# Weight buffers moved by 16 bytes under an unchanged stream of matmuls

## The reference

```python
u = rms_norm(h, g_norm) @ w_in              # 2048 x 8192, columns q, f, i, z
...
h = h + (o * jax.nn.silu(z)) @ w_out        # 2048 x 2048
...
u = rms_norm(h, g_kv) @ w_kv                # 2048 x 4112
...
sub = jnp.einsum("thpc,hpnc->thpn", qh, peer_sub_keys)
v1, i1 = lax.top_k(sub[:, :, 0], 16)
...
h = jnp.einsum("cd,chkd->chk", xc, jnp.take(peer_u, ec, axis=0))
a = jax.nn.gelu(h, approximate=False) * gc
y = jnp.einsum("chk,chkd->cd", a, jnp.take(peer_v, ec, axis=0))
```

## The kernel before

| tensor | byte | modulo 64 |
|---|---|---|
| `e_coef_hi` | 22240 | 32 |
| `wlo`, `raw` | 24416 | 32 |
| `gap` (unused, 576 bytes) | 57184 | 32 |
| `token` | 57760 | 32 |
| `whi` | 57856 | 0 |
| `hT` | 74240 | 0 |
| `xb` high, low | 91648, 109056 | 0, 0 |
| `xa` high, low | 126464, 143872 | 0, 0 |
| `e_coef_lo` | 144128 | 0 |
| `e_coef_first` | 228096 | 0 |

## Time and profile before

### The profile page before, as it was taken

How to read it: one execution, slowest core, us unless ns; L and a number is a source line. 1 busy time by engine, 2 the same in 40 slices (tenths; PEclk the granted TensorE clock), 3 DMA queues, 4 the chain that set the end, 5 groups by cost and what they waited for, 6 DMA issues and landing times.

```text
span 3083.3 us, 63457 instructions
## 1 busy us (share of the span) xinstructions
PE 3026.1 (98%) x25252; PEld 2947.4 (96%) x25252; DVE 1885.8 (61%) x3274; ACT 1629.6 (53%) x2604; POOL 667.0 (22%) x292
## 2 busy tenths in 40 slices
PE   8999999999999999989999999999999999999999
PEld 7999998999999998869999989999999999999999
DVE  5555556744544558767777788654457865554554
ACT  5766766566678743565444443444444444444443
POOL 3333333444444333214444400000000000000000
PEclk9999999999999999999999999999999999999999
DMA  5444443454444454415555544555554455555554
GB/s 192 148 139 147 141 145 123 168 175 164 164 139 145 139 184 150 137 55 191 178 179 185 182 138 139 187 185 187 189 190 165 152 180 190 189 181 188 190 190 163
DMA packets 72288, 506.67 MB, mean 164 GB/s; under 512 B 7904, under 2 KB 10464, under 8 KB 11232
## 3 DMA queue, kind: packets, MB, share of 16 engines
q1 hardware_dynamic: 71584, 503.16, 47.8%
q10 hardware_dynamic: 576, 1.72, 0.2%
HBM read 502.75 MB, written 2.10 MB: 164 GB/s over the span
## 4 chain that ended last, share of the span: by engine, by line
PE 92%; DVE 5%; ACT 2%; issue 1%; DMA 0%; SPq 0%; DVEq 0%; ACTq 0%
PE bank L451 12%; PE bank L452 12%; PE bank L453 12%; PE bank L465 5%; PE bank L2285 4%; PE banks L2285 4%; PE bank L2286 4%; PE banks L2286 4%; PE bank L2287 4%; PE banks L2287 4%; PE banks L2061 3%; PE banks L2062 3%; PE banks L2063 3%; PE bank L2061 2%; PE bank L2062 2%; PE bank L2063 2%
## 5 line engine op out<-in xcount | busy, mean ns | idle before, releaser
L428 ACT ACTIVATE whi<-raw 128x1024 fp32r<-128x1024 f32 x898 | 941.1, 1057 | 970.2 <-PE bank L453 391.4
L435 DVE TENSOR_TENSOR wlo<-raw,whi 128x1024 fp32r<-128x1024 f32 x667 | 820.1, 1241 | 446.5 <-ACT whi L428 445.3
L435 POOL TENSOR_TENSOR wlo<-raw,whi 128x1024 fp32r<-128x1024 f32 x231 | 610.1, 2642 | 965.1 <-ACT whi L428 965.0
L451 PE MATMUL bank<-xa_hi,whi 128*128 128x272 f32 (+1 forms) x2000 | 582.3, 291 | 7.0 <-DVE wlo L435 5.7
L452 PE MATMUL bank<-xa_lo,whi 128*128 128x272 f32 (+1 forms) x2000 | 572.2, 286 | 0.0
L453 PE MATMUL bank<-xa_hi,wlo 128*128 128x272 f32 (+1 forms) x2000 | 571.1, 286 | 0.0
L451 PEld LDWEIGHTS bank<-xa_hi,whi 128*128 128x128 f32 x2000 | 375.8, 188 | 12.6 <-issue 7.5
L452 PEld LDWEIGHTS bank<-xa_lo,whi 128*128 128x128 f32 x2000 | 377.1, 189 | 1.3
L453 PEld LDWEIGHTS bank<-xa_hi,wlo 128*128 128x128 f32 x2000 | 376.0, 188 | 0.0
L451 PE MATMUL bank<-xb_hi,whi 128*128 128x256 f32 (+1 forms) x1120 | 318.4, 284 | 1.5 <-DVE wlo L435 1.5
L452 PE MATMUL bank<-xb_lo,whi 128*128 128x256 f32 (+1 forms) x1120 | 316.3, 282 | 0.0
(11 more groups left out here) (443 smaller groups left out, 6732.6 us busy)
## 6 DMA issues: line engine op xcount, KB each, us to landing
raw<-in_w SPq DMA_DIRECT2D x251, 1024.0 KB, 4.8
raw<-in_v SPq DMA_DIRECT2D x128, 1024.0 KB, 5.2
raw<-in_u SPq DMA_DIRECT2D x96, 1024.0 KB, 4.8
hT<-in_hT SPq DMA_DIRECT2D x4, 544.0 KB, 8.2
out<-hT SPq DMA_DIRECT2D x8, 256.0 KB, 2.3
r_keys<-in_keys ACTq DMA_DIRECT2D x1, 1024.0 KB, 4.7
c_mask<-in_masks ACTq DMA_DIRECT2D x1, 320.0 KB, 2.7
g_mask<-in_masks SPq DMA_DIRECT2D x1, 272.0 KB, 12.2
```

The source lines that it names most:

```text
L428: act.activation(whi[:, (2 * t.q + half) % 4, :], raw[:, t.q, half * 1024:(half + 1) * 1024], ACT.Copy).then_inc(w_hi_done, 1)
L435: eng.tensor_tensor(wlo[:, t.q, at], raw[:, t.q, at], whi[:, slot, :].bitcast(F32), ALU.subtract).then_inc(w_lo_done[half], 1)
L451: te.matmul(ps, hi, x[0][:, kk, cols], start=(kk == 0), stop=False)
```

## The change

A helper, `line_on`, declares a tensor with 16 bytes (`LINE` = 4 floats) more on either side and returns the part behind the first 16. `wlo`, `raw` and `whi` are declared through it. `gap` becomes 64 bytes smaller, so that `hT` and all that follows keep their addresses.

```diff
 STEP = 8
+LINE = 4
 N_ACT = 18
...
         sq2 = tensor(ctx, "sq2", [P, 2, L])
+        def line_on(name, stack, n, dt=F32):
+
+            room = tensor(stack, name, [P, 4 * n + 2 * LINE], dt)
+            return room[:, LINE:LINE + 4 * n].rearrange("p (a b) -> p a b", a=4)
+
         with ExitStack() as st:
-            wlo = tensor(st, "wlo", [P, 4, D], F32R)
-        raw = tensor(ctx, "raw", [P, 4, D])
-        tensor(ctx, "gap", [P, P + 16])
+            wlo = line_on("wlo", st, D, F32R)
+        raw = line_on("raw", ctx, D)
+        tensor(ctx, "gap", [P, P + 16 - 4 * LINE])
         token = tensor(ctx, "token", [P, 24])
-        whi = tensor(ctx, "whi", [P, 4, D // 2], F32R)
+        whi = line_on("whi", ctx, D // 2, F32R)
         hT = tensor(ctx, "hT", [P, KT, L])
```

## The result

The changed kernel takes 3113.95 us (3112.35 to 3114.88), the kernel before 3085.57 beside it (3082.94 to 3087.09). The ratio is 1.0091, 95% interval 1.0078 to 1.0103: slower by 0.9%, where 0.5% faster was forecast. The profiled execution spans 3113.1 us, 29.8 more than before. The granted clock is 0.995 in both.

The account below looks back on a forecast made before the run. TensorE's matmul pace was taken to bound the kernel. Gains of 9.8 us (256-wide projections), 5.9 us (272-wide) and 0.2 us (first tiles) sum to 15.9 us off the 3085.7 us median: 3069.8 us, range 3046 to 3115.

Parts of the forecast that it names:

- TensorE's pace is all there is to gain or lose: Whole kernel: TensorE busy 3026.1 of 3083.3 us, no bubbles to win, only the pace from matmul to matmul left.
- The place of operands sets the pace: Matmul triples: where moving operand and weights lie is worth up to 2.5 ns in 117.
- The measure, distance modulo 64: Triples: moving operand's place less that of weights loading beside it, modulo 64 bytes; triples with nothing at 0 run faster.
- Rival A: All triples: place doesn't matter in 16-byte steps, or gains and losses cancel; 3085.7 us, within 6 us; chance 0.27.
- Down projections 0 us: Down projections, 6048 matmuls at 116.3 ns: no member stands at 0, so nothing changes; 0 us.
- Projections -9.8 us at 256 columns, -5.9 us at 272: Projections: triples without a 0 save 1.0 ns on 9792 matmuls and 1.1 ns on 5328.
- First tiles -0.2 us: First tiles of the two down projections: 96 matmuls gain 2.5 ns each, 0.2 us.
- Float32 matmuls, copies, loads and waits 0 us: L465, L428, L435, loads into `raw` and TensorE's waits: durations stay or have room to spare; 0 us.
- Rival C: Loads into `raw`: destination off 32 bytes doubles them, the load sets the pace, about 10% more, 3394 us; chance 0.02.
- B: Triples: slower, the first tile's pattern spreads and down projections lose their good place; 3091.7 to 3124 us; chance 0.31.
- half-way form: Weight rows off a 32-byte boundary touch 17 pieces, not 16: 0.5 ns on 21168 matmuls, 11 us, 3096.7; within B's 0.31.
- D: Projections and down projections: 16 bytes apart beats 32, 37.8 us gained, 3048 us; chance 0.10.

Follow-up runs that it names:

- m1: Small kernel with only TensorE at work, not computing the reference: 83 groups of 96 triple matmuls, each at its own operand places; 985.02 us.
- m2: Small kernel, only TensorE at work: 256 pairs of places of `whi` and `wlo` under a 256-wide projection, plus forms with all operands shifted together; 3091.82 us.
- e4: Kernel before with `wlo`, `raw` and the three coefficient tensors at +16 bytes, `whi` at -240, x unmoved; 3113.31 us, ratio 1.0089.
- e3: Kernel before with weights unmoved, `e_coef_hi` at +16 and `e_coef_lo` at +240 bytes; 3093.99 us, ratio 1.0028.
- e7: Changed kernel with `coef_hi` alone moved, to 256 modulo 512; 3101.19 us, ratio 1.0048.
- m4: Small kernel, only TensorE at work: 256 pairs of places of `coef_hi` and `coef_lo` under a down projection, weights as before; 2984.00 us.

## Why the prediction was wrong, point by point

**TensorE's pace is all there is to gain or lose: right.** After the change the same chain holds, TensorE has no new gaps, and the sum of paces gives 27.4 of 29.8 us.

**The place of operands sets the pace: right**, and now shown with TensorE alone at work. My reading of the Trainium skill (SBUF — State Buffer, section Who interferes with whom), that places would not matter, falls with `m1`.

**The measure, distance modulo 64: wrong.** This is where the forecast turned around. I had three triples (0, 32, 0 twice and 32, 32, 32), whose three paces fit the tale "what stands at 0 is slow", and read the untried 16 and 48 as good because they aren't 0. Rival A had noted that 0, 32, 0 gives both 117.3 and 118.8. In `m1` neither 32 nor 64 is a period, in `m2` a projection's form with all distances kept gave 117.2 and 118.9 in turn, in `e4` unchanged distances gave 118.5 and not 116.3, and in `e3` the distances of after gave 117.8 and not 120.0.

**Down projections 0 us ("have no 0 to lose"): the failed step.** They lost 3.70 ns on 6048 matmuls, 22.4 us, most of the whole. They had a good place to lose: about thirteenth of 256. Of the 44.3 us between the forecast (-15.9) and the result (+28.4) these are 22.4; 15.5 more are in the 256-wide projections and 5.2 in the 272-wide ones.

**Projections -9.8 us at 256 columns, -5.9 us at 272: wrong in sign for the first, in size for the second.** 117.52 became 118.10 (+5.7 us) and 125.25 became 125.11 (-0.7 us). First tiles -0.2 us: 118.8 became 118.2, 0.1 us.

**Float32 matmuls, copies, loads and waits 0 us: right,** with 216 ns, 1057, 1242 and 2640 ns, 5.3 us and 7.8 us. That 216 ns are two passes of 108, and 108 a floor, was a reading of one number; no run tests it, and no group of a triple ran below 113.3. Rival C is out.

**Rivals.** B came nearest: down projections lose their good place. That a meeting of two reads is behind it is not shown, and neither a finer nor a longer distance turned out to be the measure. Its half-way form, a price for weight rows off a 32-byte boundary, is out with `e3`, where none is off and 1.5 ns are lost. A and D are out with the result; whole steps of 16 bytes change the pace from 113.3 to 120.0 in `m1`. B's steps of price were too mild for the down projections (117.3, or 118.8 for everything; they came to 120.0) and too harsh for the rest, so that 3114 lies between its 3091.7 and its 3124. What I ought to have weighed is what a move of a good place means. When 116.3 is the fastest pace that any 256-wide triple of the trace shows and the rule behind it isn't known, the likelier way for it is up. The range reached 3115 and the result is 1 us inside, which is luck rather than care; the chance of 0.33 for slower was too low.

## What to carry to other kernels

When a kernel is bound by back-to-back matmuls with a weight load beside each, the places of moving operand and weights can be worth some per cent: 113.3 to 122.2 ns for one shape here, 3066.90 to 3123.04 us for this kernel with nothing moved but two small tensors. They shift whenever a tensor ahead of them is resized. Compare such kernels by matmuls per us in a stretch where TensorE never idles, and suspect the places if the granted clock and the busy times of the other engines are the same and only PE's grows. Don't work out the good places from a modulus: scan them with the matmuls alone, start each candidate in several ways, and time the best in the kernel, since a placement's pace in a small kernel need not be its pace there (115.6 against 117.8 in `e7`).

## What the runs showed of the hardware that I had not expected

- The pace of one float32r form (256 columns, weights loaded for each) takes values from 113.3 to 122.2 ns in steps of 16 bytes (`m4`), and 123.3 and 126.7 ns with the moving operands 4 or 8 bytes off (`m1`).
- The absolute place counts too: a projection's form with all operands moved together runs at 117.2 ns at 0, 32 and 64 bytes and at 118.9 at 16 and 48 (`m2`).
- One placement can have two or three rhythms (113.3 or 118.9; 116.3, 117.8 or 118.5), and which one it falls into was not predictable here; others held one behind 8 or 16 different lead-ins (120.0, 122.2).
- Float32 matmuls kept their 216 ns when their weights moved by 16 bytes, and a load with its destination off a 32-byte boundary takes about the time it took (5.3 us against 5.2).

What in TensorE or in its reads makes these rhythms stays open. The runs show where it is, not how it works.
